# Second block of a two-block transformer kernel: attention in head pairs beside the mLSTM's projections, the scan of both directions in step beside the gates' projections

## What is computed

```python
def hybrid_layer(x, ctx, ..., last):
    xn = rmsnorm(x, norm_g) * (1 + scale_x) + shift_x      # the same for ctx
    aq, ak, av, az, mq, mk, mv, mo, mz, mi, mf = project(xn, w_in)
    # 8 heads of 64 over 2 key heads, rope, window of 128 plus all of the context, a sink
    att_x = window_ctx_attention(q, k, v, kc, vc, sink) * silu(az)
    # mLSTM: 4 heads of 128; q and k pass a 5-tap depthwise convolution and silu
    h_ctx, ctx_state = mlstm_bidir(cq, ck, cmv, cmi + b_i, cmf + b_f, init)
    h_lat, _ = mlstm_bidir(xq, xk, mv, mi + b_i, mf + b_f, ctx_state)
    m_x = rmsnorm_per_head(sigmoid(mo) * h_lat) * silu(mz)
    x = x + gate_x * (concat(att_x, m_x) @ w_out)
    # not in the last layer: the same for ctx
```

```python
dmat = where(lower, b[:, None] - b[None, :] + ii[None, :], -inf)
qk   = (q @ k.T) * exp(dmat - m_t)
num  = w_inter * (q @ C) + qk @ v;  den = w_inter * (q @ n) + qk.sum(-1)
h    = num / max(|den|, exp(-m_t))
C    = a * C + (w * k).T @ v;       n = a * n + (w * k).sum()
```

## Time and profile before

| | us |
|---|---|
| median of three runs | 2448.18 |
| the profiled execution | 2445.93 |
| its span, first to last instruction | 2444.1 |
| PE busy (share of span) | 2205.6 (90%) |
| DVE busy | 691.0 (28%) |
| ACT busy | 369.2 (15%) |
| mean granted clock of TensorE | 0.949 |

### The profile page before, as it was taken

The page is one execution under the profiler, slowest core; times in us unless marked ns, Lnnn a source line. Parts: engine busy times, 40 slices in busy tenths (PEclk is TensorE's granted clock), DMA queues, the critical chain, the costliest instruction groups (busy, mean ns, idle before and its releaser), DMA issues.

```text
span 2444.1 us, 34578 instructions
## 1 busy us (share of the span) xinstructions
PE 2205.6 (90%) x14880; PEld 1533.5 (63%) x14880; DVE 691.0 (28%) x1680; ACT 369.2 (15%) x894; POOL 24.3 (1%) x16
## 2 busy tenths in 40 slices
PE   7799999998899999999999999889986778998766
PEld 6668888785776566666666666437464454486455
DVE  2932000265311111111111111224027663232754
ACT  1132000104210000000000000120124230112331
POOL 1010000000000000000000000000000000000000
PEclk9999999998899999999999999999998889998778
DMA  8463444245249999999999999602210001122000
GB/s 291 155 225 128 148 154 155 104 155 207 69 170 420 420 420 421 420 420 420 420 421 420 420 416 417 266 35 86 86 52 1 1 1 69 69 104 86 0 1 17
DMA packets 71930, 506.59 MB, mean 207 GB/s; under 512 B 7776, under 2 KB 9824, under 8 KB 11232
## 3 DMA queue, kind: packets, MB, share of 16 engines
q1 hardware_dynamic: 69296, 497.18, 51.3%
q0 software_dynamic: 1152, 4.19, 0.7%
q10 hardware_dynamic: 1328, 2.97, 0.3%
HBM read 503.27 MB, written 1.05 MB: 206 GB/s over the span
## 4 chain that ended last, share of the span: by engine, by line
PE 56%; DMA 10%; DVE 7%; ACT 2%; issue 1%; SPq 0%; DVEq 0%; ACTq 0%
PE ps L377 54%; DMA ring<-weights 9%; DMA work<-weights 1%; PE ps L931 1%; DVE small L1941 1%; ACT work L1278 1%; DVE work L1406 1%; DVE work L1936 1%; DVE work L1858 0%; PE ps L603 0%; DVE work L1811 0%; DVE work L1802 0%; DVE work L1410 0%; DVE work L1906 0%; DVE work L1844 0%
## 5 line engine op out<-in xcount | busy, mean ns | idle before, releaser
L377 PE MATMUL ps<-work 128*32 128x256 f32 (+6 forms) x5464 | 569.1, 398 | 52.0 <-DMA ring<-weights 15.3
L377 PE MATMUL ps<-work,ring 128*128 128x256 f32 (+1 forms) x2048 | 575.8, 442 | 25.8 <-DVE work L1722 12.1
L377 PE MATMUL ps<-xc,ring 128*128 128x256 f32 x2368 | 520.6, 381 | 8.2 <-DVE xc L1418 7.1
L377 PEld LDWEIGHTS ps<-work,ring 128*128 128x128 f32 x2048 | 391.3, 192 | 206.1 <-issue 150.3
L377 PEld LDWEIGHTS ps<-xc,ring 128*128 128x128 f32 x2368 | 450.8, 191 | 82.3 <-DMA ring<-weights 11.3
L377 PEld LDWEIGHTS ps<-work 128*32 128x32 f32 (+3 forms) x5464 | 325.9, 127 | 228.5 <-issue 135.1
L377 PE MATMUL ps<-ring,work 128*32 128x256 f32 (+3 forms) x3832 | 407.0, 437 | 8.5 <-ACT work L1088 6.5
L377 PEld LDWEIGHTS ps<-ring,work 128*32 128x32 f32 (+1 forms) x3832 | 224.2, 123 | 141.9 <-issue 91.1
L1612 DVE TENSOR_TENSOR work<-work,ps 128x256 f32<-128x256 f32 x42 | 17.7, 421 | 455.0 <-ACT work L1182 455.0
L377 PE MATMUL ps<-work,con 128*128 128x256 f32 (+1 forms) x278 | 95.6, 497 | 41.3 <-DVE work L1444 13.7
L1182 ACT ACTIVATE work<-ps 128x256 f32<-128x256 f32 x42 | 16.1, 384 | 638.1 <-PE ps L377 638.1
(11 more groups left out here) (218 smaller groups left out, 1129.8 us busy)
## 6 DMA issues: line engine op xcount, KB each, us to landing
ring<-weights SPq DMA_DIRECT2D x303, 1024.0 KB, 17.5
work<-weights SPq DMA_DIRECT2D x168, 1024.0 KB, 22.0
work<-rel POOLq DMA_DIRECT2D x8, 512.0 KB, 11.4
con<-consts ACTq DMA_DIRECT2D x1, 1368.0 KB, 10.2
xc<-x_t SPq DMA_DIRECT2D x1, 1024.0 KB, 7.5
xc<-ctx_t ACTq DMA_DIRECT2D x1, 1024.0 KB, 21.5
out<-work SPq DMA_DIRECT2D x1, 1024.0 KB, 3.9
par<-params SPq DMA_DIRECT2D x1, 872.0 KB, 9.0
```

The costliest lines, as they stand in the source:

```text
L377: ins = eng.matmul(o, lhs, rhs, start=start, stop=stop, **kw)
```

## The change

The first projections are only those of attention (`block2_first`: aq, ak, vg, rope, az). Attention then works on pairs: the two heads whose queries lie in partitions 0 to 63 and 64 to 127, for one query tile, in one round (16 pairs in layer 0, 8 in layer 1, each with four rounds of run-out). PE issues both scores next to each other into banks 3 and 4, and the value products of the two heads in turn; DVE adds the mask and takes the maximum of both in one instruction; for `ctx` tiles the copy is gone and ACT's exponential reads PSUM. After each round PE issues a share of pieces of the k, q and v projections of the mLSTM (`block2_second`, banks 0 and 1); a piece is two 512-column or four 256-column matmuls. DVE runs slices of the convolution after each attention round. Then the scan runs both directions in step (`mlstm`, 24 yields), with pieces of the mz and mo projections between (`block2_third`, banks 6 and 7; seven pieces ahead of the scan in layer 0, six in layer 1). Keys are turned once per token tile, ahead of the steps, and copied by ACT. `inter` and `intra` of both directions use banks 4 and 5. The last step's state change, which nothing reads, is left out. ACT copies mz and mo as they are and takes their Silu and Sigmoid in one instruction each after the scan. The line order of the weight units follows.

```diff
-UNITS_IN2 = ["mq", "mq", "mk", "mk", "vg", "mv", "mv", "aq", "aq", "ak", "az", "az", "mz", "mz", "mo", "mo"]
+UNITS_IN2 = ["aq", "aq", "ak", "vg", "az", "az", "mk", "mk", "mq", "mq", "mv", "mv", "mz", "mz", "mo", "mo"]
+CHUNKS2 = [4, 5, 6, 7, 0, 1, 2, 3]
...
+        mix2 = [azs[:, c, :] for c in range(CC)] + [xn[:, c, :] for c in range(CC, KC)]
...
+        prob2_flat = hs.rearrange("p a b -> p (a b)")
+        pt2_flat = mos.rearrange("p a b -> p (a b)")
...
+        inter_s = (first_inter_s, last_inter_s)
...
+        def att_pairs(l):
+            return [(l, i, qt) for i in range(CC) for qt in range(4 if l == 0 else 2)]
+
+        def att_rounds(l):
+            return len(att_pairs(l)) + 4
...
+        SCAN_YIELDS, SCAN_START = 4 * 6, {0: 7, 1: 6}
...
+            def pieces(key, o, lhs, rhs, bank):
+
+                n = o.shape[-1]
+                for c in range(KC):
+                    last = mm(o, lhs(c), rhs(c), c == 0, c == KC - 1)
+                    if c == KC - 1:
+                        last.then_inc(bank_full[bank], 1)
+                        finished[key] = now[0]
+                    if (c + 1) % (2 if n > T else 4) == 0:
+                        yield
...
+                for k, c in enumerate(CHUNKS2):
+                    if k % 2 == 0:
+                        w = next_unit()
+                    o = fill(("pre", l, c), k % 2, (s["pre_copied"], 8 * l + k + 1))
+                    yield from feature_pieces(("pre", l, c), w, (c % 2) * P, o, n_q if c < M_HEADS else 2 * T, k % 2)
...
+                    o = fill(("mz", l, c), 6 + c % 2, (s["mz_copied"], 4 * l + c + 1))
+                    yield from feature_pieces(("mz", l, c), w, (c % 2) * P, o, n_q, 6 + c % 2)
...
+            def block2_attention(l):
...
+                        k = ATT[item]
+                        eng.wait_ge(s["att_prob"], k)
+                        for half in range(2):
+                            o = fill(("at",) + item + (half,), 5 + half, (s["att_turned"], 2 * k - 1 + half))
...
+                    if n < len(items):
+                        _, i, qt = items[n]
+                        k = ATT[items[n]]
+                        keys = slice(0, 2 * T) if qt < TT else slice(T, 2 * T)
+                        cols = slice(0, 2 * T) if qt < TT else slice(0, T)
+                        read_by = (s["att_scored"], k) if qt < TT else (s["att_exp"], 2 * k)
+                        for half in range(2):
+                            p0 = DH * half
+                            o = fill(("as",) + items[n] + (half,), 3 + half, read_by)
+                            mm(o[:, cols], aq[p0:p0 + DH, i, qt * P:qt * P + P], ak[p0:p0 + DH, keys], True, True)\
+                                .then_inc(bank_full[3 + half], 1)
+                    if 3 <= n < len(items) + 3:
+                        _, i, qt = items[n - 3]
+                        k = ATT[items[n - 3]]
+                        eng.wait_ge(s["att_turned"], 2 * k)
+                        b = 2 if i % 2 else 7
+                        if qt == 0:
+                            o2 = fill(("ao", l, i), b, (s["att_out"], CC * l + i + 1))
+                        kts = 4 if qt < TT else 2
...
+                                at = (2 * (k % 2) + half) * 2 * T + kt * P
+                                last = mm(o2[DH * half:DH * half + DH, qt * P:qt * P + P],
+                                          vtok[:, vt, DH * half:DH * half + DH], pt2_flat[:, at:at + P],
...
+            def attention_beside_projections(l):
+                attention, rest = block2_attention(l), block2_second(l)
+                rounds, total = att_rounds(l), 48 if l == 0 else 40
+                for n in range(rounds):
+                    now[0] = n
+                    next(attention)
+                    for _ in range(share(n, rounds, total)):
+                        next(rest)
...
+                def inter(j, d):
+                    t = ORDER[d][j]
+                    eng.wait_ge(s["state_out"], state_no(l, j - 1, d))
+                    for half in range(2):
+                        o = fill(("inter", l, j, d, half), 4 + half, (s["inter_scaled"], ROW[l, j, d]))
+                        for h in range(2):
...
+                def intra(j, d):
+                    t = ORDER[d][j]
+                    eng.wait_ge(s["qk_turned"], ROW[l, j, d])
+                    for half in range(2):
+                        o = fill(("intra", l, j, d, half), 4 + half, (s["mh_num"], ROW[l, j, d]))
...
+                eng.wait_ge(s["cqk_out"], 8 * l + M_HEADS)
+                for t in range(4):
+                    o = fill(("kt", l, t), 2 + t, (s["keys_turned"], 4 * l + t + 1))
+                    for h in range(M_HEADS):
+                        last = eng.transpose(o[:, h * P:h * P + P], cqk[:, M_HEADS + h, t * P:t * P + P], ident)
+                    last.then_inc(bank_full[2 + t], 1)
+                decay_rows(0)
...
+                        inter(j, 0)
+                    yield
+                    if rows:
+                        inter(j, 1)
+                    yield
+                    if j < 3:
+                        state_change(j, 0)
+                    if rows:
+                        turned_weights(j, 0)
+                    yield
+                    if rows:
+                        turned_weights(j, 1)
+                    yield
+                    if j < 3:
+                        state_change(j, 1)
+                    if rows:
+                        intra(j, 0)
+                    yield
+                    if j < 3:
+                        decay_rows(j + 1)
+                    if rows:
+                        intra(j, 1)
+                    yield
...
+                scan, rest = mlstm(l), block2_third(l)
+                total = (32 if l == 0 else 16) - SCAN_START[l]
+                now[0] = -1
+                next(scan)
+                for _ in range(SCAN_START[l]):
+                    next(rest)
+                for n in range(SCAN_YIELDS):
+                    now[0] = n
+                    next(scan)
+                    for _ in range(share(n, SCAN_YIELDS, total)):
...
+                            bias = rmax[:, k % 4, half:half + 1]
+                            at = (2 * (k % 2) + half) * 2 * T
+                            pr = prob2_flat[:, at:at + w]
+                            src = pr if qt < TT else tile(eng, "as", *items[n], half)[:, 0:w]
+                            eng.activation(esink[:, k % 4, half:half + 1], par[:, PC(f"sink{l}", i + CC * half)],
+                                           ACT.Exp, bias=bias)
+                            eng.activation(pr, src, ACT.Exp, bias=bias, accum_out=rsum[:, k % 4, half:half + 1])\
+                                .then_inc(s["att_exp"], 1)
...
+                for k, c in enumerate(CHUNKS2):
+                    eng.wait_ge(s["conv2_acc"], 8 * l + k + 1)
+                    n = T if l == 1 and c < M_HEADS else 2 * T
+                    eng.activation(cqk[:, c, 0:n], cqk[:, c, 0:n], ACT.Silu, bias=par[:, PC(f"conv_b2{l}", c)])\
+                        .then_inc(s["cqk_out"], 1)
+                for t in range(4):
+                    o = tile(eng, "kt", l, t)
+                    eng.activation(k_tok[:, t, :], o, ACT.Copy).then_inc(s["keys_turned"], 1)
...
+                    eng.activation(wt, ex, ACT.Exp).then_inc(s["stats_exp"], 1)
+                    eng.wait_ge(s["stats_exp"], k)
...
+                    if rows:
+                        for d in range(2):
+                            for h in range(M_HEADS):
+                                n = 4 * d + h
+                                ins = eng.activation(decay[:, n, :], amask[:, n, :], ACT.Exp, bias=nm_row[:, n:n + 1])
+                            ins.then_inc(s["decay_out"], 1)
+                        inter(0)
+                    yield
+                    if rows:
+                        inter(1)
                     yield
                     yield
...
+                eng.wait_ge(s["mo_copied"], 8 * l + 2 * q_tiles)
+                eng.activation(mos[:, 0:q_tiles, :], mos[:, 0:q_tiles, :], ACT.Sigmoid).then_inc(s["mos_out"], 1)
+                eng.wait_ge(s["mz_copied"], 4 * (l + 1))
+                n_q = 2 * T if l == 0 else T
+                eng.activation(mzs[:, :, 0:n_q], mzs[:, :, 0:n_q], ACT.Silu).then_inc(s["mzs_out"], 1)
...
+                    yield "pre", l, c2 + 1
...
+                        if tap < CONV_K2 - 1:
+                            yield "more",
...
+                    eng.wait_ge(s["keys_turned"], 4 * l + ORDER[d][j] + 1)
+                    for h in range(M_HEADS):
+                        ins = eng.tensor_scalar(kw[d][:, h, :], k_tok[:, ORDER[d][j], h * P:h * P + P],
+                                                wt[:, 2, 4 * d + h:4 * d + h + 1], SC, ALU.mult, ALU.mult)
...
+                    statistics(j)
+                    eng.wait_ge(s["stats_exp"], step_no(l, j))
+                    if j < 3:
```

(57 more changed lines are left out.)

651 lines of the change are left out of this document (299 added, 352 removed).

## The result

The changed kernel takes 2315.4 us (median of 4 runs, 2312.8 to 2323.2) where the kernel before takes 2448.2: ratio 0.946, 95% interval 0.945 to 0.947, a gain of 132.8 us where 160.3 were forecast. The time lies within the range; the predicted 2288 is 27 us too low. The range held by its width: its upper part was there for two rivals that did not come, and the loop over ACT that cost most of the time is in no rival.

What follows compares the result with a forecast made beforehand. Projections were bound by PE's work, interleaved scan and attention by hand-offs. Overlaying them takes layer 0 from 415.2 to 320.3 us and layer 1 from 298.9 to 233.5, gaining 160.3: forecast 2288, range 2248 to 2336.

Steps and rivals of the forecast that it cites:

- First stretches: Attention's projections (aq, ak, vg, rope, az) at the start of each layer: 72.6 us in layer 0, 45.4 in layer 1.
- Second stretch: Attention pairs beside the mLSTM's k, q and v projections: 126.2 us in layer 0, 98.5 in layer 1.
- Is PE really the bound here?: Check on layer 0's attention rounds: PE's round about 6.3 us, DVE's mean 6.1, just under it.
- start of 3 us a layer: Attention beside projections: az's last Silu, two table loads and the first pair's chain precede the first probabilities, 3 us.
- rival (b): Attention rounds: DVE and hand-offs bound them, 8 us a wide round against 6.3; +16, 2304 us; chance 0.15.
- Rival (a): Attention pairs do not overlap: 17.3 us of scores, 17.5 of values return; 2323, or 2305 for scores alone; chance 0.2.
- Third stretch, layer 0: Scan beside z and o projections: 121.5 us, PE standing some 5.5 us before each second inter product.
- Rival (c): Scan: the stop at the inter banks is hidden, 5.5 us less a step, about -22, 2266 us; chance 0.1.
- Third stretch, layer 1: Scan beside z and o: 89.6 us, statistics starting at 18.9, two steps without rows at 13 each.
- Rival (d): Stretches two and three: TensorE drops to 1.2 GHz, 363 us of work doubles, 2651 us; chance 0.02.
- (e): The stretches do not overlap at all, attention's steps standing behind pieces: about the old time; chance 0.01.
- 1.5 us each: Layer 0's scan: clock loss after each of PE's short stops before the second inter product, 6 us in all.

Runs made afterwards that it cites:

- the kernel with the order put right: Changed kernel with one yield moved, so ACT copies a projection tile after the round's exponentials, not before: 2295.9 us.
- all four edits: Changed kernel, copies after exponentials, inter product before decay exponentials, pieces moved into PE's stop, layer 1 Silus first: 2253.9 us; with three pieces before layer 1's scan, 2248.8.
- the reordering: Changed kernel with ACT scaling the first direction's inter product ahead of the eight decay exponentials instead of behind them: 2293.9 us.
- the kernel with the pieces placed: Changed kernel with the same z and o projection pieces per step, three of them ahead of the second inter product where PE stopped: 2286.0 us.

## Why the prediction was right, and where it was off

- **First stretches**, +3.5 and +3.3 us. The records were priced at the full rate. Behind the norm, PE starts at the 1.2 GHz level; busy time by stretch in layer 0, kernel after, then before (the granted clock is the third number from the end):

```profile
1613.40:1616.40 3.00, 3.00 (x4) 1.45 (x5) 3.00 (x7) 1.83 (x4) 0.00 (x0) 0.50 0.00 0
1616.40:1619.40 3.00, 3.00 (x5) 1.17 (x5) 2.60 (x7) 1.80 (x3) 0.00 (x0) 0.60 0.00 0
1619.40:1622.40 3.00, 3.00 (x8) 1.33 (x7) 0.00 (x0) 0.00 (x0) 0.00 (x0) 1.00 0.00 0
```

```profile
1605.70:1608.70 3.00, 2.99 (x4) 1.44 (x5) 3.00 (x7) 1.84 (x4) 0.00 (x0) 0.52 0.00 0
1608.70:1611.70 3.00, 3.00 (x8) 1.33 (x7) 2.60 (x7) 1.80 (x3) 0.00 (x0) 1.00 0.00 0
```

  3.00 at 0.50 and 3.00 at 0.60 lose 1.5 and 1.2 us; 0.8 us of standing ahead of the first scores is the rest. Before, the same start lost 1.4. Layer 1's start has the same clock (0.50 and 0.59) and 0.9 us of standing.
- **Second stretch, the step that failed.** "Is PE really the bound here?" was answered from PE's and DVE's work per round, and ACT was passed over with "ACT has 4.3 us a round": busy time, not order. The prediction does not say where the projection copies stand in ACT's round; they are of the same round as the exponentials, and stand ahead of them. The stretches are 13.9 us in layer 0 and 1.3 in layer 1 above the forecast, but the order costs more: 15.5 and 5.2 us against the kernel with the order put right (19.5 by the medians). The forecast was too high elsewhere by 1.6 and 3.9 us, which hid part of it: its start of 3 us a layer measured 1.1 in layer 0 (PE busy 123.44 of 124.60) and none in layer 1 (94.6 of 94.6 in the kernels with all four edits). It is not rival (b): DVE's wait is a consequence of ACT's, and without it DVE's 71.7 us in the stretch hide beside PE's.
- **PE's prices in it** held. Scores overlap fully; a wide pair takes 1.06 us, of which two records at 0.430 are 0.86 and the rest, 0.20, comes with the change of tile shape (0.15 was taken). Sixteen value records take 1.03 us to the next start, half of 1.74 and 0.16. Rival (a) is false. By the Trainium skill, "TensorEngine Tiling (Array Packing)", Key Properties, tiles work in parallel and a change of mode drains the engine. The rows agree: two scores take no longer than one, and the 0.20 and 0.16 us at a change of shape fit a drain.
- **Third stretch, layer 0**, 122.0 for 121.5. The chain up to the inter banks was right (8.8 us for 9.2), and so were the stop (4.5 to 5.6 us for 5.5) and its cause. Rival (c) describes not this kernel but what could be had: for its 22 us the reordering gave 21.5 and the pieces 29.5. That 22 and 21.5 agree is chance, since the reordering left 2.2 to 3.3 us of each stop in layer 0 and gained from the slow records that went.
- **Third stretch, layer 1**, 97.2 for 89.6, sizes. Statistics start at 21.9 us (18.9 forecast), since behind the wait for the late Silus the transposes and decay rows ran slow, 2.6 us of the 3.0; the two steps without rows take 16.7 and 14.5 us for 13 (2196.84 to 2213.49 to 2227.96, starts of the statistics), where PE stands 6.47 and 4.53 us behind the keys.
- **The clock.** Rival (d) did not come: 0.84 is the lowest of the six stretches. Nor did (e): even with attention apart from the projections the time is 2368.6. The term "1.5 us each" for the short stops was of the right size (0.9 and 0.5 us on the first two runs behind one stop), but in layer 1's two steps without rows only the decay rows were priced at a low clock. They ran at the full rate (1.88 us for four records); the product and the piece behind the stops were slow (2.06 and 3.62 us, for 1.13 and 1.89).

The sum: 13.9 + 1.3 for the second stretches, 6.8 for the first, 8.1 for the third, 30.1 in all against 27.4 by the medians. The profiled execution is 37.6 us above the 2285.6 forecast for it, the other 7.5 being the late start of its second block; the other three executions, 6 to 10 us shorter, have no profile.

## What to carry to other kernels

Where generators interleave two streams, write down for each engine the order within one round and ask of every copy whether what it waits for is made earlier or later in that round than what stands behind it: the engine with the least work can close the loop. Put filler work where the chain stops an engine, not evenly over the steps; the same pieces gave 29.5 us more by their place alone. And allow for a stop of PE to cost more than its length: here 1.5 to 2.6 us more where the granted clock fell behind it.

## What the runs showed of the hardware beyond expectation

- Two scores of 64 rows and 512 columns in the two row halves take 1.06 us from start to next, one alone 1.05.
- A stand of 4.34 us cost 6.9, and one of 4.49 another 1.5 beyond itself (2.06 for 1.13, 2.41 for 1.88). That is in part why the gains expected as 13, 18 and 3 us came out as 21.5, 29.5 and 8.8. The length of the stand alone does not tell: behind stands of 2.17 and 3.31 us the granted clock stayed at 1.00, behind one of 2.60 it was 0.65 for 4.1 us, and behind two of 1.27 and 0.61 us, a transpose run apart, it was 0.58 in the changed kernel and 1.00 at the same place in the kernel with the pieces placed.
- Value products of the column halves cost 1.09 us for sixteen alternating and 1.58 head by head; eight cost 0.66 us either way.
